# Decoder step on one NeuronCore: where the norm's second statistics, the lower halves of split operands and the convolution's first and last steps stand

## The chip, the cores and the metric

The kernel runs on one core of a Trainium2 chip. The metric is the device time of one execution in microseconds, the median of the runs shown. TensorE (PE), VectorE (DVE), ScalarE (ACT), GpSimd (POOL) and SyncE (SP) each take their instructions in order and wait for each other through semaphores.

## The reference

One inference step of a four-layer decoder for 512 prompt rows and 64 sample rows (8 x 8), 576 rows of width 1024 in all, in float32. Layer 0 and 3 mix with a gMLP, layer 1 with a convolution module, layer 2 with multi-head latent attention; each mixer and each SwiGLU is followed by a norm with conditioning (adaLN):

```python
for i in range(DEPTH):                       # mixer: gmlp, conv, mla, gmlp
    x = LN(ALPHA * x + g1 * mixer(x * (1 + a1) + s1))
    x = LN(ALPHA * x + g2 * (silu(h @ wg) * (h @ wu)) @ wd)   # h = x * (1 + a2) + s2

def conv_module(h, ctx, ...):
    a = h @ w_pw1 + b_pw1                    # 1024 -> 2048
    a = a[..., :D] * sigmoid(a[..., D:])
    full = concatenate([ctx, a], 1)          # ctx: the last 30 rows
    y = depthwise_conv(full, w_dw) + b_dw    # width 31
    y = silu(layer_norm(y, ln_g, ln_b))
    return y @ w_pw2 + b_pw2, full[:, -30:]
```

`layer_norm` takes mean and variance of each row over its 1024 elements. s1, a1, g1, s2, a2, g2 come from `silu(c) @ ada_w[i]`.

## The kernel before, in words

Activations lie transposed: `xa` holds the residual stream as 8 tiles of 128 features by 576 rows (columns 0 to 511 prompt, 512 to 575 sample). A product works on one half of the rows at a time, 288 columns: half 0, then half 1. Precision comes from splitting: a float32 operand is held as an upper part (`h_hi`, `w_hi`, `a_hi`) and a lower part (`h_lo`, ...), and a product is three matmuls for each of its eight tiles of 128 features: upper x upper, upper weights x lower activations, lower weights x upper activations. A matmul is issued through one helper (`mm`, L977), a transpose through `transposes` (L1086). Weights come by DMA in units of 128 x 1024, issued by SyncE; GpSimd splits them (L884 `w_hi`, L887 `w_lo`).

**A norm** (`down_norm` on each engine; seven in the program have it with the first products of the next stage behind it). TensorE makes the down product's eight output tiles, half 0 and half 1. VectorE adds each to `xa` (`add_norm`, L2316 to L2321), which frees its bank in PSUM. It sums tiles (`sums`, L2327) and their squares (`squares`, L2332), which ScalarE has made (L1791), in two groups of four tiles per half; TensorE adds the partial sums over the partitions by a product with a matrix of ones (in the first half it adds tile 7 from `xa` and `sq` itself). Then ScalarE takes the deviation (L1806, L1808), VectorE takes the reciprocal (L2351) and normalises (L2356, L2358), and ScalarE applies the conditioning and writes `hf` and `h_hi` (L1828). VectorE makes `h_lo` from them: for half 0 in two groups of four tiles (`first_half`, L2382), for half 1 in four pairs of tiles (`second_half`, L2392), after the sample columns (`samples`, L2373; cast L2390).

The next stage begins before the norm is done. `first_four` (TensorE) makes the first four products in parts, as tiles of `h` come: two parts of four tiles in half 0, four parts of two in half 1. Each part waits for its `h_lo`. Within a product all three kinds of matmul alternate tile by tile. After the first product of half 0's last part stands `second_stats`, the statistics of half 1, eight records in the trace (each of these matmuls leaves two). Behind half 0's products come products for the conditioning (`ada_w`), then half 1.

**The convolution** (layer 1): the products of w_pw1 come in pairs of units, one pair a tile (value and gate); after pairs 0 and 1, TensorE turns the conditioning row, the sample states `st_in` (eight groups) and the taps `wd_in`; VectorE copies them out of the banks (`stT` L2723, `wdq` L2730, `wdT` L2732) behind its gates, `ada_coefs` (L2257) and `gbw` (L2715 to L2721). ScalarE adds residuals (L1844, sixteen), and issues the DMAs that spread the taps (`w<-wdq`, L1999) and four shifted copies of each tile (`x<-full`, L2009), eight of them before the next gate. GpSimd makes `diag` from mask and taps (L896) and the samples' products (L913). TensorE then runs, for each tile m of eight: the products of pair m + 2 (while there are any), 64 tap matmuls (L977, `pb<-x,diag`), two transposes for the new state. VectorE adds bias into `yc` (L2765), and accumulates `s_sum`, `s_sq` (L2759). At the end: two `ada_conv` pairs, the convolution's statistics (`conv_stats`; the last tile from `yc`, `sqy` by TensorE) with two pairs inside, four pairs after, and `down_norm` with w_pw2. All of this order is written out by hand; a planner (`plan.product`) only counts how often each unit of weights is used.

## Time and profile before

| | |
|---|---|
| median of 3 runs | 3134.82 us (3131.73 to 3137.52) |
| the profiled execution | 3137.26 us |
| its span | 3135.5 us |
| mean granted TensorE clock | 0.989 of full |
| busy: PE, weight loads, DVE, ACT, POOL | 96%, 89%, 46%, 18%, 48% |
| DMA | 354.80 MB, mean 113 GB/s |

The profile is of one execution; its span lies within that execution's own time, and durations come from it. The granted clock is given as a share of full speed: 1.00 is 2.4 GHz, 0.50 is 1.2 GHz. Where TensorE waits, the bracket of a timeline row says how long it stood idle and what released it; the end of a matmul is modelled, so starts are firmer than ends.

### The profile page before, as it was taken

Reading aid. Unit: us, or ns where it says so; the run is one execution under the profiler, and the core shown is the slowest. Engines: PE = TensorE matmul, PEld = TensorE weight load, DVE = VectorE, ACT = ScalarE, POOL = GpSimd, SP = SyncE. Lnnn points to the kernel's source line nnn. Section 1 sums busy time; section 2 is a strip of 40 time slices with the busy share of each in tenths; the row PEclk is TensorE's granted clock in tenths of the full one; section 3 lists DMA queues with packets and bytes.
Section 4 is the critical chain, followed back from the end, with each engine's and each line's share of the span. In section 5 each row is a group of like instructions: output and inputs, shape, how many; then the busy total and the mean of one; then the engine's idle time right before and its main releaser. Section 6 shows DMA issues by size and latency. Waiting matters only on the chain.

```text
span 3135.5 us, 52792 instructions
## 1 busy us (share of the span) xinstructions
PE 3019.7 (96%) x21984; PEld 2788.6 (89%) x21984; DVE 1426.7 (46%) x2530; ACT 555.7 (18%) x1115; POOL 1502.1 (48%) x889
## 2 busy tenths in 40 slices
PE   6999999999999999999989999999999999999998
PEld 4799999999876699999976688999997999899997
DVE  3153663424654763423566546242364536634233
ACT  2230140000220340000233323000023311400001
POOL 2455445545465345555520045554544464455554
PEclk8999999999999999999999999999999999999999
DMA  6642343232345343424321334333322333222321
GB/s 237 226 121 76 121 169 123 82 121 83 90 117 157 130 173 113 145 91 159 92 61 42 104 125 167 122 132 123 127 68 81 98 89 93 69 84 85 88 82 64
DMA packets 450475, 354.80 MB, mean 113 GB/s; under 512 B 26120, under 2 KB 424832, under 8 KB 437933
## 3 DMA queue, kind: packets, MB, share of 16 engines
q1 hardware_dynamic: 435744, 324.79, 32.8%
q10 hardware_dynamic: 14493, 26.63, 2.8%
q8 instruction: 174, 2.85, 0.4%
q14 instruction: 64, 0.52, 0.1%
HBM read 337.86 MB, written 5.25 MB: 109 GB/s over the span
## 4 chain that ended last, share of the span: by engine, by line
PE 85%; DVE 7%; DVEq 2%; ACT 2%; DMA 1%; issue 1%; SPq 1%; ACTq 0%; POOLq 0%; POOL 0%
PE pb L977 83%; DVE h_lo L2382 1%; DVEq L2333 1%; DVE pb L2351 1%; DMA ada_first<-in_ada_w 1%; DVE part L2332 1%; DVE xa L2358 1%; ACT h_hi L1828 1%; ACT hf L1828 1%; PE pb L1672 0%; PE pb L1086 0%; DVEq L2357 0%; DVE h_lo L2392 0%; DVE hf L2373 0%; DVE xa L2356 0%
## 5 line engine op out<-in xcount | busy, mean ns | idle before, releaser
L884 POOL TENSOR_SCALAR w_hi<-w_raw 128x1024 fp32r<-128x1024 f32 (+2 forms) x416 | 444.0, 1067 | 1347.1 <-DMA w_raw<-in_ffn_w_up 405.1
L887 POOL TENSOR_TENSOR w_lo<-w_raw,w_hi 128x1024 fp32r<-128x1024 f32 (+2 forms) x416 | 987.2, 2373 | 69.0 <-issue 69.0
L977 PE MATMUL pb<-h_hi,w_hi 128*128 128x288 f32 x3584 | 974.8, 297 | 12.2 <-DVE h_lo L2392 7.0
L977 PE MATMUL pb<-h_lo,w_hi 128*128 128x288 f32 x3584 | 968.2, 295 | 0.0
L977 PEld LDWEIGHTS pb<-h_hi,w_hi 128*128 128x128 f32 x3584 | 674.3, 188 | 23.6 <-DVE h_lo L2392 12.0
L977 PEld LDWEIGHTS pb<-h_lo,w_hi 128*128 128x128 f32 x3584 | 675.1, 188 | 0.3
L977 PE MATMUL pb<-a_hi,w_hi 128*128 128x288 f32 x2176 | 592.8, 297 | 4.7 <-DVE a_lo L2199 3.9
L977 PE MATMUL pb<-a_lo,w_hi 128*128 128x288 f32 x2176 | 587.4, 295 | 0.0
L977 PE MATMUL pb<-h_hi,w_lo 128*128 128x288 f32 x3584 | 561.8, 295 | 0.0
L977 PEld LDWEIGHTS pb<-h_hi,w_lo 128*128 128x128 f32 x3584 | 504.9, 188 | 0.7 <-POOL w_lo L887 0.5
L977 PEld LDWEIGHTS pb<-a_hi,w_hi 128*128 128x128 f32 x2176 | 408.5, 188 | 13.2 <-issue 6.9
L977 PEld LDWEIGHTS pb<-a_lo,w_hi 128*128 128x128 f32 x2176 | 408.9, 188 | 0.7
L2541 DVE TENSOR_TENSOR pr<-pb,sg 128x288 f32<-128x288 f32 x176 | 80.1, 457 | 629.3 <-PE pb L977 601.7
L977 PE MATMUL pb<-a_hi,w_lo 128*128 128x288 f32 x2176 | 344.5, 295 | 0.2
L977 PEld LDWEIGHTS pb<-a_hi,w_lo 128*128 128x128 f32 x2176 | 307.4, 188 | 0.8 <-POOL w_lo L887 0.7
L1885 ACT ACTIVATE sg<-pb 128x288 f32<-128x288 f32 x176 | 72.2, 411 | 1330.6 <-PE pb L977 1330.5
L2317 DVE SCALAR_TENSOR_TENSOR xa<-pb,gate,xa 128x288 f32<-128x288 f32 (+1 forms) x288 | 137.9, 479 | 210.8 <-PE pb L977 210.3
L2199 DVE TENSOR_TENSOR a_lo<-pr,a_hi 128x288 fp32r<-128x288 f32 x176 | 204.6, 1162 | 15.5 <-issue 2.9
L977 PE MATMUL pb<-w_hi,h_hi 128*128 128x256 f32 (+2 forms) x416 | 135.6, 342 | 21.0 <-DVE h_lo L2392 7.9
L2316 DVE TENSOR_TENSOR pb<-pb,gate 128x64 f32<-128x64 f32 x144 | 33.2, 231 | 255.8 <-PE pb L977 254.8
L2197 DVE CAST a_hi<-pr 128x288 fp32r<-128x288 f32 x176 | 129.2, 734 | 16.1
L977 PE MATMUL pb<-w_hi,h_lo 128*128 128x256 f32 (+2 forms) x416 | 132.5, 335 | 0.0
(321 smaller groups left out, 2699.6 us busy)
## 6 DMA issues: line engine op xcount, KB each, us to landing
ada_w<-in_ada_w SPq DMA_DIRECT2D x80, 1024.0 KB, 8.1
w_raw<-in_ffn_w_gate SPq DMA_DIRECT2D x88, 512.0 KB, 3.8
w_raw<-in_ffn_w_up SPq DMA_DIRECT2D x88, 512.0 KB, 3.8
w_raw<-in_gmlp_w_in SPq DMA_DIRECT2D x64, 512.0 KB, 4.0
w_raw<-in_ffn_w_down SPq DMA_DIRECT2D x64, 512.0 KB, 3.8
w_raw<-in_gmlp_w_out SPq DMA_DIRECT2D x32, 512.0 KB, 4.4
w_raw<-in_ffn_w_down SPq DMA_DIRECT2D x32, 384.0 KB, 3.3
w_raw<-in_conv_w_pw SPq DMA_DIRECT2D x24, 512.0 KB, 4.0
```

The source lines that it names most:

```text
L884: nc.gpsimd.tensor_scalar(w_hi[:, s, 0:w], w_raw[:, s, 0:w], 1.0, 1.0, ALU.mult, ALU.mult).then_inc(split_hi, 1)
L887: nc.gpsimd.tensor_tensor(w_lo[:, s, 0:w], w_raw[:, s, 0:w], w_hi[:, s, 0:w].bitcast(F32), ALU.subtract).then_inc(split_lo, 1)
L977: return nc.tensor.matmul(out, lhsT, rhs, start=start, stop=stop)
L1828: last = fn(dst, xa[:, m, h * HALF:h * HALF + w], ACT.Identity, scale=cs[:, t % RING_T, m, 0:1], bias=cb[:, t % RING_T, m, 0:1])
L1885: fn(sg[:, q, :], pb[:, b, 0:HALF], func, **kw).then_inc(sg_ready, 1)
L2197: v.tensor_copy(hi, src)
L2199: return v.tensor_tensor(lo, src, hi.bitcast(F32), ALU.subtract)
L2316: v.tensor_tensor(bt(ps[:, HP:HALF]), bt(ps[:, HP:HALF]), gs, ALU.mult)
L2317: last_ = v.scalar_tensor_tensor(out=y, in0=ps[:, 0:w], scalar=gp, in1=y, op0=ALU.mult, op1=ALU.add)
L2332: v.reduce_sum(part[:, 1, n, half_cols(h)], sq[:, m0:m1, half_cols(h)].rearrange("p m t -> p t m"), AX.X)
L2333: dve.drain().then_inc(part_ready, 1)
L2541: v.tensor_tensor(pr[:, q, :], pb[:, (G.n + 1) % BANKS, 0:HALF], sg[:, q, :], ALU.mult).then_inc(acc_free, 2)
```

## The change

In every norm but the last: VectorE sums tiles 4 to 6 of half 1, not 4 to 7, and does so ahead of `h_lo` of the second group. TensorE adds tile 7 itself from `xa` and `sq`, for which ScalarE squares tile 7 apart. The statistics of half 1 are split: those of the first four tiles stand ahead of the next stage's products, the rest behind the upper pieces of part 0. `first_four` is regrouped: for each part all four products first do two of the three kinds of matmul, and then, in a second round, the third. In all parts but the first of half 0 the third kind is upper weights x `h_lo`, and the start of a part waits only for `h_hi` (counted by `hf_ready`, or `hs_ready` in half 1). At the very first input the same grouping holds.

```diff
+            def second_stats():
+
+
+                mean_p, sq_p = [pb[:, b, 0:HALF] for b in stat_banks[NT.n, 1]]
+                cols = half_cols(1)
+                pe.wait_ge(y_ready, YR.n + 6)
+                mm(mean_p, ones[:], xa[:, 7, cols], False, False)
+                pe.wait_ge(sq_ready, SQ.n + 7)
+                mm(sq_p, ones[:], sq[:, 7, cols], False, False)
                 pe.wait_ge(part_ready, PT.n + 4)
                 mm(mean_p, ones[:], part[:, 0, 1, cols], False, True).then_inc(mean_ready, 1)
                 mm(sq_p, ones[:], part[:, 1, 1, cols], False, True).then_inc(aux_ready, 1)
                 PT.up(4)
-                YR.up(5)
-                SQ.up(7)
+                YR.up(6)
+                SQ.up(8)
                 NT.up()
...
+                if t and h == 0:
+                    second_stats_early()
                 for part_ in range(parts):
-                    if h and part_ % 2 == 0:
-                        pe.wait_ge(h_pair, 2 * t + part_ // 2 + 1)
+                    ks = range(kn * part_, kn * part_ + kn)
+                    lower_last = h or part_
+                    lower_count = ((h_pair, 2 * t + part_ // 2 + 1) if h and part_ % 2 == 0
+                                   else (h_ready, 4 * t + 2 * h + (part_ // 2 if h else part_) + 1))
+                    if h:
+                        pe.wait_ge(hs_ready, 4 * t + part_ + 1)
+                    elif part_:
+                        pe.wait_ge(hf_ready, 6 * t + part_ + 1)
                     else:
-                        pe.wait_ge(h_ready, 4 * t + 2 * h + (part_ // 2 if h else part_) + 1)
+                        pe.wait_ge(*lower_count)
                     for i in range(4):
                         if part_ == 0:
                             if units is not None and i % 2 == 0:
                                 units(i // 2)
                             pe.wait_ge(acc_free, G.n + i + 1)
-                        last = step(i, range(kn * part_, kn * part_ + kn), (G.n + i) % BANKS)
+                        step(i, ks, (G.n + i) % BANKS, "hh", True, False)
+                        step(i, ks, (G.n + i) % BANKS, "lh" if lower_last else "hl", False, False)
+                    if t and h == 0 and part_ == 0:
+                        second_stats()
+                    if lower_last:
+                        pe.wait_ge(*lower_count)
+                    for i in range(4):
+                        last = step(i, ks, (G.n + i) % BANKS, "hl" if lower_last else "lh", False, True)
                         if part_ == parts - 1:
                             last.then_inc(acc_ready, 1)
-                            if t and h == 0 and i == 0:
-                                second_stats()
                 G.up(4)
...
@@ -2388,7 +2466,7 @@
                 dve.wait_ge(hf_ready, HF.up())
                 ms, src = slice(2 * p, 2 * p + 2), hf[:, p // 2, 2 * (p % 2):2 * (p % 2) + 2, :]
                 v.tensor_copy(h_hi[:, ms, SEQ:], src[:, :, HP:])
-                dve.drain()
+                dve.drain().then_inc(hs_ready, 1)
                 v.tensor_tensor(h_lo[:, ms, half_cols(1)], src, h_hi[:, ms, half_cols(1)].bitcast(F32),
                                 ALU.subtract).then_inc(h_ready if p % 2 else h_pair, 1)
...
@@ -2442,11 +2520,12 @@
                 first.normalise(6, KT)
                 for m in range(5, KT):
                     add_norm(e, m, 1)
-                dve.drain().then_inc(y_ready, 1)
+                    if m >= 6:
+                        dve.drain().then_inc(y_ready, 1)
+                sums(1, 4, 7, 1)
+                squares(1, 4, 7, 1, 6)
                 first_half(1)
-                sums(1, 4, 8, 1)
-                squares(1, 4, 8, 1, 6)
-                second = Stats(1, 7)
+                second = Stats(1, 8)
```

(`pieces` is the loop that issues one kind of matmul of one product for the tiles `ks`.)

In the convolution: the taps `wd_in` are turned first; the states are turned inside the third pair, whose products go unit by unit through both halves. VectorE empties the taps, then makes `gbw`, then copies the states. ScalarE issues four shifted copies, the taps' spread, four shifted copies, and then the residuals. The last tile is done in halves: taps of half 0, its statistics, then taps of half 1 and the new state rows in banks of the products' group. Tiles 6 and 7 are summed by TensorE. Three `ada_conv` pairs stand before the last tile's taps, one before the second statistics, four after. ScalarE takes half 1's deviation after four tiles of half 0; the DMAs of the new states go to the start of half 1.

```diff
+                def third_pair():
+
+
+                    for n, s in enumerate(take_units(2)):
+                        for h in range(2):
+                            at_ = G.n + 2 * h + n
+                            pe.wait_ge(acc_free, at_ + 1)
+                            last = product(pb[:, at_ % BANKS, 0:HALF], range(KT),
+                                           lambda k: (s, slice(k * P, (k + 1) * P)),
+                                           (lambda k: h_hi[:, k, half_cols(h)], lambda k: h_lo[:, k, half_cols(h)]))
+                            if n or h == 0:
+                                last.then_inc(acc_ready, 1 + n * h)
+                        if n == 0:
+                            state_turns()
+                    G.up(4)
...
-                state_turns()
+                pe.wait_ge(st_in_full, 48)
+                transposes([(k * CW, wd_in[:, k * P:(k + 1) * P]) for k in range(KT)])
+                third_pair()
                 for m in range(KT):
-                    if m < KT - 2:
+                    if 0 < m < KT - 2:
...
+                    if m == KT - 1:
+                        pe.wait_ge(acc_free, G.n + BANKS)
+                        ada_conv_pairs(3)
                     pe.wait_ge(diag_ready, m + 1)
                     pe.wait_ge(x4_full[m % 2], 16 * QT * (m // 2 + 1))
+                    last = tap_products(pb[:, aux_bank(), :], m, 0, SEQ if m < KT - 1 else HALF)
                     last.then_inc(aux_ready, 1)
                     X.up()
...
-                pe.wait_ge(acc_free, G.n + BANKS)
-                ada_conv_pairs(2)
-                for h in range(2):
-                    conv_stats(h, 2 * (h == 0))
+                    if m < KT - 1:
+                        new_rows(pb[:, aux_bank(), :], m).then_inc(aux_ready, 1)
+                        X.up()
+                conv_stats(0)
+                tap_products(pb[:, G.n % BANKS, :], KT - 1, HALF, SEQ).then_inc(last_tile, 1)
+                new_rows(pb[:, (G.n + 1) % BANKS, :], KT - 1).then_inc(last_tile, 1)
+                ada_conv_pairs(1)
+                conv_stats(1)
                 ada_conv_pairs(4)
...
-                act.wait_ge(bias_ready, 1)
-                residuals(2 * l)
-                act.wait_ge(wd_ready, 1)
-                for q in range(QT):
-                    act.dma_start(w4[:, q], wdq[QC * q:QC * (q + 1)]).then_inc(w4_in, 16)
...
-                for m in range(2):
-                    spread(m)
+                spread(0)
+                act.wait_ge(wd_ready, 1)
+                for q in range(QT):
+                    act.dma_start(w4[:, q], wdq[QC * q:QC * (q + 1)]).then_inc(w4_in, 16)
+                spread(1)
+                act.wait_ge(bias_ready, 1)
+                residuals(2 * l)
...
+                    cols = slice(0, TOK) if m < KT - 1 else half_cols(0)
+                    fn(sqy[:, m % 2, cols], yc[:, m, cols], ACT.Square).then_inc(ysq_ready, 1)
+                deviation("conv", 0)
+                act.wait_ge(yc_ready, KT + 1)
+                fn(sqy[:, (KT - 1) % 2, half_cols(1)], yc[:, KT - 1, half_cols(1)], ACT.Square).then_inc(ysq_ready, 1)
```

How this moves instructions is seen in the built order of each engine. VectorE in the first norm, from the last but one added tile of half 1 on (`pb` is a bank in PSUM, `part` holds the partial sums); before:

```order
L2316 TENSOR_TENSOR pb<-pb,gate 128x64
L2317 SCALAR_TENSOR_TENSOR xa<-pb,gate,xa 128x224
L2321 TENSOR_TENSOR xa<-xa,pb 128x64
L2382 TENSOR_TENSOR h_lo<-hf,h_hi 128x4x288
L2327 TENSOR_REDUCE part<-xa 128x288
L2332 TENSOR_REDUCE part<-sq 128x288
L2345 TENSOR_TENSOR pb<-pb,sqt 128x288
L2347 TENSOR_SCALAR pb<-pb 128x288
L2351 RECIPROCAL pb<-pb 128x288
```

and now:

```order
L2394 TENSOR_TENSOR pb<-pb,gate 128x64
L2395 SCALAR_TENSOR_TENSOR xa<-pb,gate,xa 128x224
L2399 TENSOR_TENSOR xa<-xa,pb 128x64
L2405 TENSOR_REDUCE part<-xa 128x288
L2410 TENSOR_REDUCE part<-sq 128x288
L2460 TENSOR_TENSOR h_lo<-hf,h_hi 128x4x288
L2423 TENSOR_TENSOR pb<-pb,sqt 128x288
L2425 TENSOR_SCALAR pb<-pb 128x288
L2429 RECIPROCAL pb<-pb 128x288
```

The two reduces stand ahead of `h_lo`, and only then come the second half's variance, clamp and reciprocal. TensorE at the second statistics of the same norm, the end of the first product's second part; before:

```order
L977 MATMUL pb<-h_lo,w_hi 128x288
L977 MATMUL pb<-h_hi,w_hi 128x288
L977 MATMUL pb<-h_lo,w_hi 128x288
L977 MATMUL pb<-h_hi,w_lo 128x288 x4
L977 MATMUL pb<-part,ones 128x288 x4
L977 MATMUL pb<-h_hi,w_hi 128x288
L977 MATMUL pb<-h_lo,w_hi 128x288
L977 MATMUL pb<-h_hi,w_hi 128x288
```

and now, from the down product's last piece:

```order
L980 MATMUL pb<-a_hi,w_lo 128x288 x8
L980 MATMUL pb<-part,ones 128x288 x2
L980 MATMUL pb<-h_hi,w_hi 128x288 x4
L980 MATMUL pb<-h_lo,w_hi 128x288 x4
L980 MATMUL pb<-h_hi,w_hi 128x288 x4
L980 MATMUL pb<-h_lo,w_hi 128x288 x4
L980 MATMUL pb<-xa,ones 128x288
L980 MATMUL pb<-sq,ones 128x288
L980 MATMUL pb<-part,ones 128x288 x2
L980 MATMUL pb<-h_hi,w_lo 128x288 x16
L980 MATMUL pb<-h_hi,w_hi 128x288 x4
```

The four matmuls with ones have become two ahead of the products and four behind the upper pieces of part 0; the `h_lo` pieces of part 1 (sixteen, not shown) end half 0. ScalarE at the convolution's start, from the gates of tile 1; before:

```order
L1907 ACTIVATE sg<-pb,par 128x288 x2
L1844 ACTIVATE xa<-xa,ab,ag 128x288 x16
L1999 DMA w_122<-wdq 128x1x64 x4
L2009 DMA x_119<-full 128x1x540 x8
L1907 ACTIVATE sg<-pb,par 128x288 x2
L2009 DMA x_119<-full 128x1x540 x4
```

and now:

```order
L1981 ACTIVATE sg<-pb,par 128x288 x2
L2078 DMA x_119<-full 128x1x540 x4
L2083 DMA w_122<-wdq 128x1x64 x4
L2078 DMA x_119<-full 128x1x540 x4
L1918 ACTIVATE xa<-xa,ab,ag 128x288 x16
L1981 ACTIVATE sg<-pb,par 128x288 x2
L2078 DMA x_119<-full 128x1x540 x4
```

The shifted copies of tile 0 have passed the residuals and the taps' spread, and the residuals stand behind all of them.

## Rows read from the trace of the kernel before

**Rows 1.** The page: busy time of the engines; shares of the chain that ended last.

```profile
PE 3019.7 (96%) x21984; PEld 2788.6 (89%) x21984; DVE 1426.7 (46%) x2530; ACT 555.7 (18%) x1115; POOL 1502.1 (48%) x889
...
PE 85%; DVE 7%; DVEq 2%; ACT 2%; DMA 1%; issue 1%; SPq 1%; ACTq 0%; POOLq 0%; POOL 0%
```

**Rows 2.** TensorE's waits: releaser: us in total, times, longest us.

```profile
PE pb L977 <- DVE h_lo L2392: 14.9, 11, 4.7
PE pb L977 <- DVEq L2333: 13.6, 14, 2.5
PE pb L977 <- DVE h_lo L2382: 8.8, 6, 6.9
...
PE pb L977 <- DVE xa L2321: 4.9, 7, 0.8
...
PE pb L977 <- issue: 3.1, 1, 3.1
PE pb L977 <- DMA ada_conv<-in_ada_w: 3.1, 3, 1.4
...
PE pb L977 <- DVEq L2784: 0.8, 1, 0.8
```

**Rows 3.** Timeline, TensorE, norms: start us, us, operation [idle before <-releaser].

```profile
1578.20 0.39 PE L977 MATMUL pb<-w_hi,h_hi 128*128 128x256 f32 x1 [2.13 <-DVE h_lo L2392]
...
2681.72 0.40 PE L977 MATMUL pb<-h_hi,w_hi 128*128 128x288 f32 x1 [0.55 <-DVE h_lo L2382]
...
2689.07 0.29 PE L977 MATMUL pb<-h_hi,w_hi 128*128 128x288 f32 x1
...
2690.65 1.13 PE L977 MATMUL pb<-part,ones 128*128 128x288 f32 x4
2693.01 1.24 PE L977 MATMUL pb<-part,ones 128*128 128x288 f32 x4 [1.23 <-DVEq L2333]
...
2703.66 0.61 PE L977 MATMUL pb<-h_hi,w_hi 128*128 128x288 f32 x1 [4.68 <-DVE h_lo L2392]
```

**Rows 4.** The same, VectorE, last norm.

```profile
2685.88 2.82 DVE L2382 TENSOR_TENSOR h_lo<-hf,h_hi 128x1152 fp32r<-128x1152 f32 x1
2688.63 2.25 DVE L2327 TENSOR_REDUCE part<-xa 128x288 f32<-128x1152 f32 x1
2690.81 2.12 DVE L2332 TENSOR_REDUCE part<-sq 128x288 f32<-128x1152 f32 x1
2694.31 0.47 DVE L2345 TENSOR_TENSOR pb<-pb,sqt 128x288 f32<-128x288 f32 x1 [1.39 <-PE pb L977]
...
2702.85 0.76 DVE L2392 TENSOR_TENSOR h_lo<-hf,h_hi 128x576 fp32r<-128x576 f32 x1
```

**Rows 5.** Groups by form: busy us, mean ns | idle before.

```profile
L2327 DVE TENSOR_REDUCE part<-xa 128x288 f32<-128x864 f32 x7 | 8.0, 1145 | 0.8
```

**Rows 6.** Stretches: us, busy (x) of PE, PEld, DVE, ACT, POOL, PEclk, DMA share, GB/s.

```profile
877.00:896.00 19.00, 14.56 (x93) 13.72 (x93) 11.32 (x32) 8.90 (x17) 7.78 (x7) 0.82 0.60 158
1014.00:1024.00 10.00, 6.88 (x54) 2.08 (x46) 9.67 (x9) 0.68 (x1) 9.67 (x6) 0.83 0.64 216
1040.00:1048.00 8.00, 6.58 (x30) 3.18 (x31) 5.34 (x8) 5.51 (x10) 0.00 (x0) 0.57 0.27 114
1575.00:1596.00 21.00, 16.85 (x139) 15.51 (x132) 15.69 (x39) 14.73 (x30) 1.57 (x2) 1.00 0.16 38
2702.00:2710.00 8.00, 6.33 (x27) 6.34 (x28) 6.91 (x16) 4.88 (x12) 0.00 (x0) 0.57 0.00 0
```

**Rows 7.** Timeline of the convolution's start, three engines.

```profile
879.48 0.42 PE L1086 MATMUL pb<-ident,st_in 120*128 120x120 f32 x2 [0.62 <-DVE cb L2257]
...
883.20 4.26 ACT L1844 ACTIVATE xa<-xa,ab,ag 128x288 f32<-128x288 f32 x8 [4.80 <-DVEq L2721]
...
883.72 1.86 PE L1086 MATMUL pb<-ident,st_in 120*128 120x120 f32 x8 [3.81 <-DVE stT L2723]
...
891.63 2.34 POOL L896 TENSOR_TENSOR diag<-mask,w 128x256 f32<-128x256 f32 x4 [8.58 <-DMA w<-wdq]
```

More of the change, by code:

```diff
@@ L266, in trunk @@
         gbw = ca("gbw", [P, KT, NC])
-        ci = Place(a_at, size([P, 2, QT, XW]), "conv-in")
+        ci = Place(a_at + size([P, 2, QT, XW]), 2 * size([P, DEC_B, DEC_T, CW]), "conv-in")
         wd_in = ci("wd_in", [CW, D])
@@ L1141, in second_stats, with pieces @@
                 PT.up(4)
-                YR.up(5)
-                SQ.up(7)
+                YR.up(6)
+                SQ.up(8)
                 NT.up()
+            def pieces(out, ks, w_at, a_at, w, wait, start, end, w_moves):
+                for k in ks:
+                    s, cols = w_at(k)
+                    wait(s)
+                    a = a_at(k)
+                    lhsT, rhs = (a, w[:, s, cols]) if w_moves else (w[:, s, cols], a)
+                    last = mm(out, lhsT, rhs, start and k == 0, end and k == KT - 1)
+                return last
             def first_four(t, h, step, units=None):
@@ L1177, in first_halves, with step, w_at @@
                 first_four(t, h, step, None if h else lambda _: slots.extend(take_units(2)))
             def first_tokens(t, h, slots, widths, both):
-                def step(i, ks, b):
+                def step(i, ks, b, kind, start, end):
                     blk, tt = ((0, 2), (0, 3), (0, 4), (1, 2))[i] if h else divmod(i, 2)
                     n = widths[blk]
+                    def w_at(k):
+                        return slots[blk][k // 4], slice(k % 4 * n, (k % 4 + 1) * n)
                     if tt == TT - 1:
-                        if KT - 1 not in ks:
+                        if not end or KT - 1 not in ks:
@@ L1194, in units @@
+                    w, wait = (w_lo, wait_lo) if kind == "lh" else (w_hi, wait_hi)
+                    a_at = token_parts(h_hi, h_lo, both, tt)[kind == "hl"]
+                    return pieces(pb[:, b, 0:n], ks, w_at, a_at, w, wait, start, end, True)
                 def units(blk):
@@ L1453, in state_turns, with tap_products, new_rows @@
                 def state_turns():
-                    pe.wait_ge(st_in_full, 48)
                     for k in range(KT):
                         transposes([(n * 4 * CTX, st_in[:, n, k * P:(k + 1) * P]) for n in range(2)])
-                    transposes([(k * CW, wd_in[:, k * P:(k + 1) * P]) for k in range(KT)])
+                def third_pair():
[11 more added lines that the diff above has]
+                    G.up(4)
+                def tap_products(out, m, c0, c1):
+                    for g in range(TG):
+                        for q in range(QT):
+                            last = mm(out[QC * q:QC * (q + 1), 0:c1 - c0], diag[:, m % 2, q, g, :],
+                                      x4[:, m % 2, q, QT * g + c0:QT * g + c1], g == 0, g == TG - 1)
+                    return last
+                def new_rows(out, m):
+                    pe.wait_ge(full_ready, m + 1)
+                    nc.tensor.transpose(out[0:CTX, 0:P], full[:, m % 3, SEQ:SEQ + CTX], ident[:]
+                                        ).then_inc(taps_done, 1)
+                    return nc.tensor.transpose(out[0:NS, P:2 * P], snew[:, m % 3, :], ident[:])
                 slots = []
@@ L2733, in conv @@
                 dve.drain().then_inc(wd_ready, 1)
-                v.memset(full[:, :, 0:CTX], 0.0)
-                v.memset(full[:, :, CTX + SEQ:SAMPLES], 0.0)
+                v.tensor_tensor(gbw[:], gate[:, 2 * l % RING_T], par[:, C_PW2:C_PW2 + KT].unsqueeze(2)
+                                .to_broadcast([P, KT, NC]), ALU.mult)
+                dve.drain()
+                v.tensor_tensor(ab[:, 2 * l, :], ab[:, 2 * l, :], gbw[:, :, 0], ALU.add)
+                v.tensor_tensor(gbw[:, :, 1:], gbw[:, :, 1:], gbw[:, :, 0:1].to_broadcast([P, KT, NC - 1]),
+                                ALU.subtract)
+                dve.drain().then_inc(bias_ready, 1)
                 v.memset(s_sum[:], 0.0)
                 v.memset(s_sq[:], 0.0)
+                for m in range(KT):
+                    v.tensor_copy(stT[:, m, :], pb[:, aux(), 0:DEC_B * CTX]).then_inc(aux_free, 1)
                 dve.drain()
@@ L2784, in lower @@
                     dve.drain().then_inc(a_ready, 2)
-                first = Stats(0, 1)
-                first.invert()
-                second = Stats(1, 2)
                 for p in range(4):
```

131 lines of the change are left out of this document (69 added, 62 removed).

## The prediction

> **What bounds the kernel now.** I read the page first: busy shares and the chain of waits. TensorE is busy 96% of the span and carries 85% of the chain; VectorE carries 7% of it [rows 1]. So only places where TensorE stands still, or runs at its lower clock, can be won. The second view is the table of TensorE's waits [rows 2]. The named waits that this change can touch are in the norms (the second statistics, L2333; the lower parts h_lo, L2392 and L2382; the banks that xa frees, L2321) and in the convolution (stT, taps that wait for x, ada_conv, L2784). The third is the timeline of one norm, on TensorE [rows 3] and on VectorE [rows 4]: the 2.82 us h_lo of the second group of tiles and two reduces over four tiles, 2.25 and 2.12 us, stand one behind the other before the second statistics can close, at 2693.01. Everything of the second half (deviation, reciprocal, normalising, h_lo) hangs on that, and TensorE, which runs out of first-half products, stands 4.68 us until 2703.66. The fourth is the table of stretches with the granted clock [rows 6]: a stretch loses its length times (1 - clock). 2702 to 2710 at 0.57 lost 3.4 us, behind that 4.68 us stand.
>
> **The norms (seven times).** The waits: seven second-statistics waits, 1.23 us the last [rows 3], 9.3 us in all; the other seven of L2333's fourteen stand elsewhere in the norm and stay; h_lo L2392, 14.9 us in 11 waits; h_lo L2382 without the 6.9 us at the program's start, 1.9 us [rows 2]. Together 26.1 us. A wait costs a little on top: from start to start the stand is longer than its bracket (2690.65 with its four records of 0.24, to 2693.01, is 1.4, not 1.23). I take 0.25 us each, 4.5 us for the 18 that go.
>
> What comes in. (a) TensorE sums tile 7 itself: two matmuls with ones more for the second half, two records each. The four records behind 2693.01 take 1.24 us with the modelled end of the last; start to start I take 0.24 a record [rows 3]: 0.97 us a norm, 6.8 us. This is on the path, since TensorE is the bound. (b) The two early statistics move ahead of part 0. No work is added, and they fill the L2382 wait, 1.9 us in all; where there is none they come from behind it and cost nothing. (c) The bank wait L2321 (4.9 us, seven times) stays: the first product now does two pieces instead of three before it wants the second bank, but starts later by the early statistics; I add 1.1 us. (d) VectorE's reduces cover three tiles, 1.15 us instead of 2.2 each [rows 5], and stand before h_lo of the second group. h_lo of the second group started at 2685.88, behind the last add; from there the two reduces are done at about 2688.2. TensorE starts part 0 at about 2682.3, behind the early statistics, and has 32 records of 0.13 (twelve take 1.58, 2689.07 to 2690.65 [rows 3]), about 1 us of bank wait and two of the new matmuls before it needs them, so to 2688.0: I put 0.2 us of wait, 1.4 us in seven. The squares of tile 7 come right behind those of 4 to 6 on ScalarE, inside that time. mean_ready comes about 5 us sooner, but VectorE then still owes h_lo: free at 2688.2 + 2.8 = 2691.0, where it began the second half's chain at 2694.31 [rows 4]. The chain comes 3.2 us sooner. (e) In the second half the lower parts are asked for last, so a part starts 0.76 us (one h_lo) before it could [rows 4]: 4.0 us in all. TensorE itself arrives about 1 us sooner. So most of the eleven L2392 waits vanish; of the 4.68 about 1.8 is left, of the others together 2.2: 4.0 us.
>
> Balance: 26.1 + 4.5 - 6.8 - 1.1 - 1.4 - 4.0 = 17.3 us. The clock: the 2702 stretch lost 3.4 us [rows 6] and should go with its stand cut to 1.8 us. The first input gains 0.3 us, its lower parts behind the upper. **Norms 21.0 us.**
>
> A 2 us stand need not lower the clock: 1575 to 1596 holds one of 2.13 us [rows 3] at clock 1.00 [rows 6].
>
> **The convolution's start.** TensorE waits 0.62 us for cb and 3.81 us for stT [rows 7], because VectorE makes gates, coefficients and gbw before it empties the banks of the turned states, and 877 to 896 at 0.82 loses 3.4 us [rows 6]. With the states turned inside the third pair's products, with VectorE free for them by then, the waits go: 4.4 + 0.5 for the restarts + 3.4, less 1.0 for the wait that I leave (VectorE must empty the banks of eight turned groups while the third pair's products need theirs): **7.3 us**. The shifts: four x<-full go ahead of w<-wdq, and the sixteen residuals behind both. GpSimd's diag waited 8.58 us for w<-wdq there [rows 7] and TensorE has the third pair's 96 records of 0.13 and the turns, 14 us, before the first taps, so I put this at nothing; if that cover were gone, it would cost what ScalarE's queue is late: eight residuals took 4.26 us [rows 7], so sixteen are 8.5.
>
> **Its end.** Taps of tile 7 waited 3.1 us ("issue", for x), ada_conv 3.1 us in three, L2784 0.8 us [rows 2], with five restarts, 1.2 us; the clock lost 1.7 us (1014 to 1024) and 3.4 us (1040 to 1048) [rows 6]. Three of the ada_conv pairs now stand in the x wait. Waits, restarts and clock are 13.3 us. Against it: eight more records for tile 6's sums, 1.9 us; a wait of about 2.5 us before w_pw2's second half, whose chain on VectorE (second deviation, reciprocal) comes forward less than TensorE does; two more table loads on ScalarE beside that wait, of which I count 0.3 as seen; 1.3 us of small waits around the halved tile. Halving the taps adds no columns, and no price of its own. **7.3 us.**
>
> The sum is 21.0 + 7.3 + 7.3 = 35.6 us. The profiled execution took 3137.26 us (span 3135.5), 2.4 above the median of the three runs, 3134.82; against the median the sum gives **3099 us**. SP's and GpSimd's instructions are not moved.
>
> **Where the trace is silent.** Whether the regrouped pieces keep 0.131 us a record: the bounds are 0.13, the pace of a product's part now (a gain is excluded, since the alternating pieces keep that pace already: those twelve records are of such a product), and 0.24, a record of ones; I take 0.13, since each of those products already ends with a run of four of one kind at that pace. Whether new small waits lower the clock: 0 to 3.4 us a place.
>
> **A rule against one step.** Between 877 and 896 the clock was low beside stands of 0.62 and 3.81 us with only transposes between [rows 6, 7]; the trace cannot say which of them did it. The Trainium skill, "TensorE: Matmul & The Clock Gate", Part 4: PE-mode transpose, says that transposes do not count as a busy TensorE in the same way. By the forecast the clock gain at the conv start is 3.4 us; by that rule sixteen turns could still bring a fall, and nothing of it would come.
>
> **Rivals.**
> 1. *VectorE stays the bound of the second half* (0.17). For: its long operations stand close [rows 4]. If h_lo of the second group and the gates' products delay the chain so that it is 1 us sooner, not 3.2, then L2392 keeps some 11 us instead of 4.0, and the 3.4 us of clock stay: 3099 + 7 + 3.4 = 3109. Against: nothing is added to VectorE's queue and 2.1 us leave it.
> 2. *The clock falls elsewhere* (0.18). The 2.5 us before w_pw2's second half, 1.8 us at 2700 and the conv's turns are candidates, 1.7 to 3.4 us each. One or two: 3102 to 3106; all: 3108.
> 3. *Slower: small waits lower the clock in every norm* (0.04). Place: the first products, now cut by a bank wait, a wait for the reduces and one for h_lo within about 8 us. Before, three ada_conv stands of 3.1 us together [rows 2] had a half-clock stretch beside them, at 1040 to 1048. Price: 3.4 us a stretch of 7 us [rows 6], 24 us in seven norms, which brings 3123; the kernel is slower than before by over 6 us once each norm loses 6 us, that is once each stretch is 12 us long. The Trainium skill, the same page, "A second HAM failure mode: psum-queue depth-cycling", tells of short idle spells between matmul groups that make the clock swing without one long one. Against: each norm has three or more such waits now, and the clock over 2702 is low behind a 4.68 us stand.
> 4. *The statistics do not come sooner* (0.05): second_stats sits in TensorE's queue between products, so if it stands there for ScalarE's squares or the reduces as long as before (1.3 us), 6.8 us of new records buy nothing, and the norms give 3 instead of 21: 3117. With the convolution's new order also failing (its waits moved to tile 0's taps, 14 us back) it is 3131, no change.
>
> **Numbers.** Forecast case 3092 to 3104: 0.56. The range takes in rivals 1 and 2 and, below, the left-over waits all gone: 3087 to 3113. 0.2% is 6.3 us, about what a measurement of this kernel can tell. Faster 0.91 (forecast, rivals 1, 2, most of 4), same 0.05, slower 0.04.
>
> **What would show it.** In the waits table L2333's successor falls from 13.6 to under 6 us, h_lo L2392's from 14.9 to about 4; stT and x waits are gone; matmuls with ones gain 28 records in the norms and 8 in the convolution; a new wait of 2 to 3 us stands before w_pw2's second half; granted clock is 1.00 at 885 to 895, at the conv's end and at the last norm. I am wrong if the second half's h_lo is less than 2.5 us sooner behind the first statistics, if a regrouped product takes over 0.14 us a record, or if new stretches at half clock appear in norms.

## The result: 22 us faster where 36 were forecast, and the profile after

| | before | changed |
|---|---|---|
| median | 3136.17 us (4 runs, 3131.73 to 3138.53) | 3113.72 us (4 runs, 3109.77 to 3117.25) |
| profiled execution's span | 3135.5 us | 3114.0 us |
| mean granted TensorE clock | 0.989 | 0.991 |

The ratio is 0.9938, 95% interval 0.9927 to 0.995: faster by 16 to 23 us. The forecast was 3099, the range 3087 to 3113. The page of the changed kernel, engines and data moved, answers to [rows 1]:

```profile
PE 3020.4 (97%) x22084; PEld 2794.3 (90%) x22084; DVE 1431.8 (46%) x2529; ACT 557.7 (18%) x1125; POOL 1509.5 (48%) x889
```

TensorE's waits, answering to [rows 2] (releaser: us in total, times, longest us):

```profile
PE pb L980 <- DVE h_lo L2460: 7.0, 1, 7.0
...
PE pb L980 <- DVE a_lo L2277: 5.6, 5, 1.4
...
PE pb L980 <- DVEq L2469: 5.2, 4, 2.7
PE pb L980 <- DVE bst L2663: 5.1, 2, 3.0
PE pb L980 <- DVE xa L2399: 5.0, 7, 1.2
...
PE pb L980 <- POOL w_hi L887: 2.3, 5, 0.6
PE pb L1745 <- DMA pgr<-in_cache_krope: 2.3, 1, 2.3
...
PE pb L980 <- DVEq L2411: 2.1, 6, 0.6
PE pb L980 <- DVEq L2880: 1.9, 1, 1.9
PE pb L980 <- DVE pr L2620: 1.4, 4, 0.4
```

The second statistics' wait is gone: L2333's 13.6 us were 9.3 before the second and 4.3 before the first statistics of a half, and the 2.1 us left at L2411 all stand before the first. h_lo L2392's 14.9 us have become 5.2 us for the samples' upper half (L2469); stT's is gone. New are waits for `w_hi` and `pr`, and the waits for `a_lo` grew from 3.9 us in three to 5.6 in five.

The granted clock of some stretches (columns as in [rows 6]):

```profile
880.00:892.00 12.00, 11.81 (x91) 11.25 (x90) 7.72 (x19) 0.51 (x1) 5.34 (x6) 1.00 0.93 252
1020.00:1035.00 15.00, 14.80 (x140) 8.98 (x133) 13.20 (x20) 11.09 (x17) 6.11 (x4) 1.00 0.23 80
1782.00:1788.00 6.00, 4.68 (x29) 4.68 (x30) 2.67 (x5) 2.29 (x7) 3.57 (x2) 0.72 0.94 273
2677.00:2690.00 13.00, 10.31 (x66) 10.07 (x66) 9.68 (x22) 9.06 (x19) 0.00 (x0) 0.87 0.00 1
```

The convolution's start and end run at full clock now. The last norm still loses 13 x 0.13 = 1.7 us, and 1782 to 1788, in the sample attention's page loads, loses 1.7 that it did not lose before.

**Where the time came from.** Starts of the same TensorE operation in two traces, subtracted, give the lead over before; here at the end of each stage (times of before), for the change and for four experiments that are described below:

```
stage end (us in before)         change    e1    e2    e3   e10
 486 first norm, feed-forward      -1.3   0.5   0.0   2.0   1.8
 878 second norm                    1.3   5.1   0.2   5.5   5.0
 908 convolution's start            7.3   9.2   7.6  12.3   4.4
1060 w_pw2, second half            13.8   9.0  14.1  18.8   4.9
1194 third norm                    17.1   8.9  14.5  20.6   6.5
1539 feed-forward, layer 1         15.7   8.9  13.0  19.3   4.9
1591 fourth norm                   20.4  13.7  13.0  23.6   9.1
1866 latent attention              16.6  12.6  11.7  24.0  10.2
2317 fifth norm, feed-forward      17.7  14.7  12.4  26.2  12.5
2404 sixth norm, gMLP's start      19.8  17.2   8.5  28.4  14.9
2770 last norm, feed-forward       22.7  20.5   9.9  34.9  20.8
3093 end                           21.5  18.9   7.5  33.8  18.1
```

The convolution brought 6.0 us at its start and 6.5 up to w_pw2's second half (forecast 7.3 and 7.3). The feed-forward norms (first, third, fifth, last) brought little: -0.2 over the first (from -1.1), and 2.9 over the last where some 7 were expected. And leads are lost where the change touches nothing: 1.4 us at 1194 to 1539, 3.8 in the attention, 1.2 at the end, and 1.1 before the first norm. By these rows the norms brought 16.4 us of 20.7 (21.0 less the 0.3 for the first input), the convolution 12.5 of 14.6, and 7.5 were lost outside both.

### The profile page after: what moved, and what is told of

Its sections match the earlier page's. It is cut to its first block, busy times and chain, and to the rows that moved or that the text cites. A ratio compares the mean times of both kernels' runs of the same rounds, so it can differ in the third digit from the quotient of the medians.

```text
span 3114.0 us, 53016 instructions
## 1 busy us (share of the span) xinstructions
PE 3020.4 (97%) x22084; PEld 2794.3 (90%) x22084; DVE 1431.8 (46%) x2529; ACT 557.7 (18%) x1125; POOL 1509.5 (48%) x889
## 3 DMA queue, kind: packets, MB, share of 16 engines
q8 instruction: 175, 2.87, 0.4%
HBM read 337.86 MB, written 5.25 MB: 110 GB/s over the span
## 4 chain that ended last, share of the span: by engine, by line
issue 33%; PE 30%; POOL 24%; POOLq 10%; DVE 2%; ACT 1%; DVEq 0%; ACTq 0%
PE pb L980 29%; POOL w_lo L890 22%; POOLq L889 10%; POOL prod L916 1%; POOL diag L899 1%; PE pb L1745 0%; PE pb L1702 0%; DVE a_lo L2277 0%; POOLq L945 0%; POOL w_hi L887 0%; POOL yt L946 0%; POOL a_lo L936 0%; DVE xa L2436 0%; DVE pb L2429 0%; PE pb L1624 0%
## 5 line engine op out<-in xcount | busy, mean ns | idle before, releaser
L980 PE MATMUL pb<-h_hi,w_hi 128*128 128x288 f32 x3584 | 946.1, 296 | 10.6 <-DVE xa L2399 3.8
L980 PE MATMUL pb<-h_lo,w_hi 128*128 128x288 f32 x3584 | 927.1, 295 | 0.0
L980 PEld LDWEIGHTS pb<-h_hi,w_hi 128*128 128x128 f32 x3584 | 661.8, 188 | 21.7 <-issue 8.6
L980 PEld LDWEIGHTS pb<-h_lo,w_hi 128*128 128x128 f32 x3584 | 657.6, 188 | 0.0
L2277 DVE TENSOR_TENSOR a_lo<-pr,a_hi 128x288 fp32r<-128x288 f32 x176 | 214.5, 1219 | 13.5 <-issue 0.4
L2275 DVE CAST a_hi<-pr 128x288 fp32r<-128x288 f32 x176 | 145.9, 829 | 16.8 <-issue 0.9
L980 PE MATMUL pb<-w_hi,h_hi 128*128 128x256 f32 (+2 forms) x416 | 122.4, 343 | 15.9 <-DVE h_lo L2460 7.0
L980 PE MATMUL pb<-w_hi,h_lo 128*128 128x256 f32 (+2 forms) x416 | 114.8, 336 | 0.0
```

What stands on the lines that cost most here:

```text
L980: return nc.tensor.matmul(out, lhsT, rhs, start=start, stop=stop)
L2275: v.tensor_copy(hi, src)
L2277: return v.tensor_tensor(lo, src, hi.bitcast(F32), ALU.subtract)
```

## The first norm, read in the changed trace

ScalarE (start us, us, operation [idle before <-releaser]):

```profile
408.20 0.41 ACT L1879 ACTIVATE sqt<-pb 128x288 f32<-128x288 f32 x1 [2.67 <-PE pb L980]
409.84 0.47 ACT L1881 ACTIVATE pb<-pb,epsl 128x288 f32<-128x288 f32 x1 [1.24 <-DVE pb L2425]
415.57 1.28 ACT L1959 ACT_TABLE_LOAD   x1 [5.25 <-PE pb L980]
416.87 0.71 ACT L1959 ACTIVATE sg<-pb 128x288 f32<-128x288 f32 x2
417.46 0.57 ACT L1901 ACTIVATE hf<-xa,cb,cs 128x224 f32<-128x224 f32 x1
```

and VectorE, as it ends the first two normalised tiles, which ScalarE reads first:

```profile
413.23 0.76 DVE L2436 TENSOR_TENSOR xa<-xa,pb 128x576 f32<-128x576 f32 x1
```

In the trace of before, ScalarE:

```profile
411.24 0.41 ACT L1806 ACTIVATE sqt<-pb 128x288 f32<-128x288 f32 x1 [6.83 <-PE pb L977]
...
417.03 0.57 ACT L1828 ACTIVATE hf<-xa,cb,cs 128x224 f32<-128x224 f32 x1 [1.68 <-DVE xa L2358]
```

The statistics came early, as forecast: `sqt` at 408.20, where before it was 411.24. The changed trace is 1.1 us behind before's by then, so counted from the norm's own start they came 4.1 us sooner. But `hf` of the second half (the apply, which writes the operands of the next products) starts at 417.46, and was at 417.03 before: 0.7 us sooner by the same count. Before, it waited for VectorE; now VectorE has the two tiles ready at 414.0, and ScalarE stands 5.25 us for a gate (`sg`), whose product is now finished only in the second round of the last part, with all the others. TensorE at the end of the second half:

```profile
434.85 0.40 PE L980 MATMUL pb<-h_hi,w_hi 128*128 128x288 f32 x1 [0.36 <-DVE pr L2620]
438.83 0.37 PE L980 MATMUL pb<-h_hi,w_hi 128*128 128x288 f32 x1 [0.55 <-POOL w_hi L887]
```

and SyncE's loads and GpSimd's first split of the same timeline:

```profile
433.73 0.38 SPq L728 DMA_DIRECT2D w_raw<-in_ffn_w_up  x1
434.15 0.58 SPq L728 DMA_DIRECT2D w_raw<-in_ffn_w_gate  x1
434.78 1.14 SPq L728 DMA_DIRECT2D w_raw<-in_ffn_w_up  x1
435.96 1.65 SPq L728 DMA_DIRECT2D w_raw<-in_ffn_w_gate  x1
437.63 1.05 POOL L887 TENSOR_SCALAR w_hi<-w_raw 128x1024 fp32r<-128x1024 f32 x1 [25.27 <-DMA w_raw<-in_ffn_w_up]
```

Before, the four weight slots came free one product after another (SyncE's issues at 432.61, 433.41, 434.21, 435.01, the first split at 436.37). Now they come free almost together at the end (the issues start 0.42, 0.63 and 1.18 us apart), and TensorE waits for a bank and then for weights. That pair of waits stands behind every feed-forward norm: 0.36 + 0.55 us in brackets here, 1.2 with the restarts.

## The experiments

Each group of runs was timed beside runs of before of its own. Where a gain over the change or over e3 is given as two numbers, one is the difference of the medians and the other the difference of the distances to before.

**e1 and e2: one half of the change each.** The diff's hunks of the norms alone (`second_stats`, `first_four`, `pieces`, ScalarE's squares, VectorE's order in `down_norm`), and all others alone.

> The kernel before with the norms' part of the change alone. In the two traces the lead over before grows by about 16 us across the convolution and by only some 6 us across all norms together, where 21 were forecast. If the two parts are independent, this kernel gains 5 to 8 us (about 3129). If the small gain at the norms is an artefact of the convolution's new order upstream (weights and clock in other places), it gains 15 us or more (3121 or less).

Measured: 3118.44 us beside 3133.75 for before on that chip, ratio 0.9951 (0.9937 to 0.9964).

> The kernel before with the convolution's part alone. Independent parts: a gain of 14 to 17 us (about 3121), with the sum of this and the norms' part equal to the whole change. If the gain in the convolution needs the norms' part (its first products, its statistics), it stays under 11 us.

Measured: 3128.32 (before 3133.75), ratio 0.9987 (0.9978 to 0.9996). So 15.3 and 5.4 us, and the sum, 20.7, is about the whole; but the split is not the one that the traces led me to expect. In e2's trace the convolution does bring 14.1 us (in the table), and 6.6 of them are lost behind it. In e1's, 4.0 us come at the convolution's start, which this kernel does not touch. I come back to both.

**e3 and e4: the last part of each half, product by product.**

```diff
+                    whole = part_ == parts - 1
+                    if whole:
+                        pe.wait_ge(*lower_count)
                     for i in range(4):
...
+                        if whole:
+                            last = step(i, ks, (G.n + i) % BANKS, "hl", False, True)
+                            if part_ == parts - 1:
+                                last.then_inc(acc_ready, 1)
...
+                    if whole:
+                        continue
```

> The changed kernel, but in the last part of each half the four products are finished one after the other instead of in two rounds. Theory A (the second round is the fault: all four products, their PSUM banks and their weight slots come free together at its end; ScalarE's first gates wait for that, and the second half's apply stands behind them in its queue): 5 to 9 us faster than the changed kernel, about 3106; the waits for pr, POOL's w_hi after the norms (0.65 and 0.84 us, four times) vanish, and apply of half 1 starts about 2 us sooner behind the statistics. Rival B (the added records and the early statistics on TensorE's path are the fault, the order of the pieces is not): within 1.5 us of the changed kernel.

Measured: 3103.38 (before 3133.75), ratio 0.9904 (0.9889 to 0.9919). That is 30 us under before and 8 to 10 under the change, and theory A's signs are there. ScalarE in the first norm:

```profile
406.65 0.41 ACT L1888 ACTIVATE sqt<-pb 128x288 f32<-128x288 f32 x1 [2.67 <-PE pb L980]
410.87 1.28 ACT L1968 ACT_TABLE_LOAD   x1 [2.10 <-PE pb L980]
412.16 0.41 ACT L1968 ACTIVATE sg<-pb 128x288 f32<-128x288 f32 x1
414.05 0.41 ACT L1968 ACTIVATE sg<-pb 128x288 f32<-128x288 f32 x1 [1.47 <-PE pb L980]
414.35 0.56 ACT L1910 ACTIVATE hf<-xa,cb,cs 128x224 f32<-128x224 f32 x1
```

Apply follows the statistics by 7.7 us, not 9.3. The waits for `pr` and `w_hi` are out of the table of TensorE's waits, and the last norm's stand fell from 2.69 to 1.69 us.

> As e3, and the two early statistics stand behind the first product's first pieces, where TensorE waits for the next bank (1.46 us in the first norm). Theory A and B both: since 0.73 us of records move into a wait in seven norms, 3 to 5 us faster than e3. If the bank wait is set by VectorE alone and something else is late behind it, nothing.

Measured: 3104.15 (before 3133.75), ratio 0.991 (0.9895 to 0.9926), no different from e3. The early statistics moved into the bank wait bought nothing that can be measured; their place is not what cost the time.

**e7 and e8: the same, in one half only** (`h == 0 and ...`, `h == 1 and ...`).

> As e3, but only in the first half's last part. It makes the first gates' products ready sooner, which stand ahead of the second half's apply on ScalarE. If that queue is what counts: apply of half 1 some 2 us sooner behind the statistics, the 2.99 us stand in the last norm under 1.5 us, and 3 to 5 us of the 10 won over the changed kernel. The waits for pr and w_hi behind half 1 stay.

> As e3, but only in the second half's last part, which frees weight slots and banks one by one. If the slots are what counts: the 0.65 and 0.84 us waits in the four feed-forward norms vanish, 4.5 to 6 us won over the changed kernel; the 2.99 us stand in the last norm stays.

Measured, beside 3133.21: e7 3110.32, ratio 0.9933 (0.992 to 0.9945); e8 3105.44, ratio 0.9911 (0.9897 to 0.9925). The second half, where weight slots and banks are freed, is worth some 5 to 8 us over the change (27.8 us under before, against 22.4); in e8 the waits for `w_hi` and `pr` are gone and the longest wait for the samples' upper half (L2469 in the change) is still 2.7. The first half, ScalarE's queue, is worth little by itself (22.9 under before), though in e7's trace that stand does fall to 1.7 us and the two waits stay. So of the two ways in which the second round hurts, the slots and banks seem to weigh more; the intervals of e7, e8 and e3 are too wide to split the 10 us cleanly.

**e5 and e6: second traces** of before and of e2.

> The kernel before, unchanged, for a second trace of it. If the 7 us that the convolution's part won up to the end of the convolution (14 us) and lost again behind it are luck of single executions (TensorE's clock falls after one 3 us stand and not after another), this trace differs from the first one stage by stage by 1.7 us or multiples of it, and where its clock is low differs too. If stands decide alone, both traces have the same stretches.

> The convolution's part alone, unchanged from e2, for a second trace. Luck: the lead behind the convolution (14.1 us at its end) is lost in other places than in e2 (there 1.5 us in layer 1's feed-forward part, 2.9 in the sample attention's page loads, 3.5 before the last gMLP, 2.4 at the end). A real give-back: the same places lose the same amounts.

One execution each: 3133.34 and 3130.23 us. Both expectations were half right. The two traces of before differ by up to 5.4 us at one place and 4.0 at the end, most of it in where the clock is low: 3.4 us were lost at 1040 to 1047 in one and 1.7 in the other, nothing at 2371 in one and 1.7 in the other. But e6 loses its lead at the same places as e2 (leads 14.9, 16.2, 14.6, 11.6, 8.2, 7.1 at the stage ends 1060, 1194, 1539, 1866, 2404, 3093), and in like amounts but for the latent attention, 3.0 against 1.3. The give-back is real. Three lines of the waits of e2:

```profile
PE pb L979 <- DVE a_lo L2234: 6.6, 6, 1.3
...
PE pb L979 <- DVE bst L2619: 5.3, 2, 3.9
...
PE pb L1703 <- DMA pgr<-in_cache_krope: 2.4, 1, 2.4
```

Against before these are 2.7 us (a_lo), 0.9 (bst) and 1.6 (page loads) more; the last two stands are now long enough that the clock fell behind them in both traces, which before's did not in the first. How an a_lo wait arises is seen at the end of layer 1's feed-forward part in the changed kernel:

```profile
1485.73 2.38 POOL L890 TENSOR_TENSOR w_lo<-w_raw,w_hi 128x1024 fp32r<-128x1024 f32 x1 [0.16 <-issue]
1485.80 2.62 DVE L2277 TENSOR_TENSOR a_lo<-pr,a_hi 128x288 fp32r<-128x288 f32 x1
...
1488.48 0.41 PE L980 MATMUL pb<-a_hi,w_hi 128*128 128x288 f32 x1 [1.09 <-DVE a_lo L2277]
```

and at the same place of before:

```profile
1502.36 1.27 DVE L2199 TENSOR_TENSOR a_lo<-pr,a_hi 128x288 fp32r<-128x288 f32 x1
```

VectorE's last `a_lo` takes 2.62 us: it starts 0.07 us into GpSimd's `w_lo` and ends 0.31 behind it. Before, it took 1.27: it started 0.09 us into the `w_hi` split (1502.27 to 1503.32) and ended 0.31 behind that. Where GpSimd is idle it takes 0.46. Which of the two it meets is set by where GpSimd stands in its round; I did not find what moved GpSimd there, and made no run that moves it alone.

**e10: the mended norms without the convolution's part.**

> The norms' part alone with the last part of each half whole: e3 without the convolution's part. If the convolution's part is worth little in the whole program (5 us alone in e2): 4 to 7 us slower than e3, about 3109. If its 12 to 14 us at the place arrive once the norms are mended: 11 to 14 us slower than e3, about 3116.

Measured: 3119.27 (before 3132.49), ratio 0.9958 (0.9944 to 0.9972), 16 to 17 us slower than e3, more than the 11 to 14 expected. So the convolution's part, worth 5.4 us over before, is worth at least its full place value over the mended norms (13.3 us in e3's column); and the mending, worth 8 to 10 us over the change, is worth nothing over e1 (13.2 us under before, against 15.3). The table says where: e10 leads e1 in the feed-forward norms, and falls behind by 4.6 us at the convolution's start. VectorE there, in e1:

```profile
874.43 0.23 DVE L2759 TENSOR_TENSOR gbw<-gate,par 128x72 f32<-128x72 f32 x1
...
874.82 0.22 DVE L2763 TENSOR_TENSOR gbw<-gbw 128x64 f32<-128x64 f32 x1
```

and in e10:

```profile
874.53 1.07 DVE L2768 TENSOR_TENSOR gbw<-gate,par 128x72 f32<-128x72 f32 x1
...
875.77 2.37 DVE L2772 TENSOR_TENSOR gbw<-gbw 128x64 f32<-128x64 f32 x1
```

In e1 the weight slots come free late, GpSimd starts its splits at 875.81, behind `gbw`, and `gbw` takes 0.45 us; in before and e10 GpSimd works beside it, `gbw` takes 3.4 us, and TensorE stands 3.8 us for stT. The late slots that cost 1.2 us in each feed-forward norm happen to save 4 us here: e1 and e10 differ in the last part of each half alone. The convolution's part takes `gbw` out of TensorE's way for good, so with it that saving is no longer there to lose.

**e9: no lower part last.** `whole = h or part_`: every part but the first waits for its h_lo again.

> As e3, but each product's pieces stay together in every part but the first of half 0, so nothing is gained by asking for h_lo last. If waiting only for h_hi is worth what the forecast said (0.76 us a stand, 4 us in all, most of it in the gMLP norms and the last norm): 3 to 5 us slower than e3. If the chain's gain alone does it: within 1.5 us of e3.

Measured: 3106.87 (before 3132.49), ratio 0.9918 (0.9905 to 0.9932): 3.5 us over e3 by the medians, 4.8 by the distance to before. The intervals overlap, so this alone does not show it; size and sign are those of the forecast's 4.0.

**e12: tile 7 back with VectorE.**

```diff
-                mm(mean_p, ones[:], xa[:, 7, cols], False, False)
-                mm(sq_p, ones[:], sq[:, 7, cols], False, False)
...
-                sums(1, 4, 7, 1)
-                squares(1, 4, 7, 1, 6)
+                sums(1, 4, 8, 1)
+                squares(1, 4, 8, 1, 7)
```

> As e3, but VectorE sums four tiles again (2.2 us a reduce, not 1.15) and TensorE does not add tile 7. TensorE has 0.97 us less in each of seven norms, VectorE's chain starts 2.1 us later. If the records are the dearer side in the feed-forward norms: 2 to 5 us faster than e3. If the chain is: the statistics' wait grows by 1 us a norm and the stands of the gMLP norms and of the last by 2 us, 4 to 8 us slower.

Measured: 3124.76 (before 3132.49), ratio 0.9974 (0.9965 to 0.9983): 21 to 23 us slower than e3, far past what I expected. The first norm:

```profile
408.18 1.94 PE L980 MATMUL pb<-part,ones 128*128 128x288 f32 x4 [2.82 <-DVEq L2416]
```

TensorE now asks for the second statistics after 32 records and not after 60, so the longer reduces are in full view: 20.2 us of that wait in seven norms (none in the change), with the clock low at five of the seven. Low stretches cost this trace 15.4 us and e3's 6.8. The four records of 0.24 us buy three times their price, at this place of the statistics. Four tiles by VectorE with the second statistics asked for later, as in before, is a rival that no run here tries.

**e11: the gates apart.** As e3, and ScalarE writes the first two tiles of half 1 between the two first gates, VectorE likewise.

> As e3, and in the feed-forward norms ScalarE writes the first two tiles of half 1 between its two first gates, VectorE makes their samples and h_lo between the two gated products. If ScalarE's queue still holds the second half up (in e3 apply stands behind the gate that waits for the fourth product): the stand in the last norm falls from 1.99 to under 1 us, 1 to 2 us faster than e3. If VectorE's chain is what is last there: no change.

Measured: 3100.86 (before 3132.49), ratio 0.9901 (0.9886 to 0.9916). The stand in the last norm is gone in its trace:

```profile
2670.78 0.54 PE L980 MATMUL pb<-h_hi,w_hi 128*128 128x288 f32 x2 [0.18 <-DVEq L2482]
```

So ScalarE's queue did hold that half up. Counted from the first statistics of the same norm, the first `h_lo` of half 1 starts 38.1 us behind them in before, 36.2 in the change and 33.6 here in the first norm; 38.1, 35.6 and 32.7 in the last. By the medians e11 is 2.5 us faster than e3, by the distance to before 1.3; the intervals overlap. Both beat the change; their medians are the lowest of all.

## Why the prediction was wrong

- **The waits that go**: right. The second statistics' own wait went from 9.3 us to nothing (forecast 1.4 left), L2392's from 14.9 to 5.2 (forecast 4.0 left); bank wait 5.0 (forecast 6.0), new records 0.24 us each. That the other seven of L2333's waits stay was not quite so: 4.3 us became 2.1, since the one of 2.5 us at 1092 is not in this trace (in e3's it is).
- **"The chain comes 3.2 us sooner"**: this is one of the two places that failed. The statistics did come sooner, and VectorE's reciprocal too (410.35 against 413.31, 4.1 us from the norm's own start; `h_lo` took 1.44 us where 2.82 was counted), but I counted VectorE's queue alone. ScalarE's queue holds two gates ahead of apply, and they wait for products whose last pieces the change itself had moved to the end. Rival 1 named the gates' products, as work on VectorE and not as something that ScalarE stands for. The first `h_lo` of half 1 came 1.9 us sooner behind the first statistics in the first norm, 1.8 in the second and 2.4 in the fifth, which meets the prediction's own sign of being wrong (under 2.5). In the last norm, where 1.8 us was to be left and the clock to stay up, 2.69 us and 1.7 us of clock were seen; with the queue mended (e11) the stand is 0.18.
- **What is missing from the sum**: the regrouping signals four products at once. I priced what each part waits for, and not what waits for its end: weight slots, banks, gates. It cost 1.9 + 1.4 us of new waits behind the four feed-forward norms and, with the chain, 8 to 10 us (e3), most of the miss of 13 to 15 us. By the table of leads e3's norms bring 22.1 us, where 20.7 were forecast and the change has 16.4. Part of e3's lead in its trace is chance: it has 5.1 us less of low clock in the attention than the change, and e4 and e11, with the same last part, have the long stretch at 1590 again. The medians, and not that trace, carry the 8 to 10.
- **The clock**: low stretches between 70 and 3080 us cost 20.5 us in before and 11.9 in the change, a gain of 8.5 where the sum had 3.4 + 3.4 + 5.1 = 11.9. The stretches that I named went, but for half of the last norm's; a new one came at 1783 and the attention's grew by 1.7 us. Rival 2 held in part. The Trainium skill, "TensorE: Matmul & The Clock Gate", Part 4: PE-mode transpose, says that a transpose does not count as a busy TensorE in the same way; that the turned states lower the clock by that, no run here shows: 880 to 892 of the changed kernel has sixteen of their records between products at 1.00.
- **The convolution**: start 6.0 for 7.3, end 6.5 for 7.3 and the 1.9 us wait before w_pw2's second half for 2.5. Nearly right at its place; what is lost behind it (6.6 us in e2) was no term of the sum, and stays open: it lies in `a_lo` waits, page loads and the clock, and no run moves one of them alone. The stand at gbw was read as VectorE's order, and it was also GpSimd's work beside it.
- **Rivals 1, 3 and 4**: half 1 was held up as rival 1 has it, with L2392's successor at 5.2 us and not 11, and by ScalarE's queue and not VectorE's; no norm fell to half clock as a whole; the statistics came early.

## What to carry to other kernels

When pieces of several products are regrouped so that a late operand is asked for last, ask first who waits for each product's end. Keep the last part product by product: e3, which does so, keeps the gain and loses the new waits. And a part of a change that is measured alone may show another part's accident: here the convolution's part and the whole last part were each worth 0 to 5 us alone and 8 to 17 us beside the other.

## What the runs showed of the hardware

- Some of VectorE's operations take two to ten times as long beside some of GpSimd's: `gbw` 0.22 against 2.37 us, `a_lo` 0.46 against 2.62. What counts is where they start. Over the fourteen traces all 748 `a_lo` (128x288) that started inside a `w_lo` ended 0.31 or 0.32 us behind its end, after 1.92 to 2.65 us, and the 1245 that started inside no operation of GpSimd took 0.46. The six `gbw` of 128x64 that started inside a `w_lo` ended 0.08 us behind it (0.22 alone). So such an operation gets about its own time, less 0.15 us, once `w_lo` is done. The products `pr` out of PSUM took 0.46 inside a `w_lo` too (948 of them), and the reduces over three tiles 1.12 to 1.17. A VectorE duration from one trace is a duration beside a given neighbour.
- The same shortened the second `h_lo` of a norm, which took 2.82 to 2.85 us in each of the seven before and takes 1.36 to 1.44 now; the forecast had counted 2.82. Before, it started 0.8 us into a `w_lo` and ended 1.2 us behind it, its 1.36 less 0.15, all seven times. In the change it starts ahead of `w_lo`, beside `w_hi` alone, or in the last 0.23 us of a `w_lo`; the first norm, before and now:

```profile
402.51 2.41 POOL L887 TENSOR_TENSOR w_lo<-w_raw,w_hi 128x1024 fp32r<-128x1024 f32 x1 [0.16 <-issue]
403.30 2.84 DVE L2382 TENSOR_TENSOR h_lo<-hf,h_hi 128x1152 fp32r<-128x1152 f32 x1
```

```profile
405.28 2.39 POOL L890 TENSOR_TENSOR w_lo<-w_raw,w_hi 128x1024 fp32r<-128x1024 f32 x1 [0.16 <-issue]
407.44 1.44 DVE L2460 TENSOR_TENSOR h_lo<-hf,h_hi 128x1152 fp32r<-128x1152 f32 x1
```

- Whether the clock falls behind one stand of TensorE is not fixed by its length in the middle range. Over the fourteen traces, stands (start to start) between 70 and 3080 us had a stretch at 1.2 GHz begin during them or within 2 us behind in 23 of 23 cases from 3.9 us up, in 11 of 15 from 3.2 to 3.7, in 21 of 35 from 2.5 to 3.2, and in 1 of 17 from 2.2 to 2.5; of 28 from 1.9 to 2.2 us long 8 had, some of them with other stands close by. Behind the same stand the same kernel's clock fell in one trace and not in the other (3.26 us at 2370 in before's first, 2.87 at 2365 in its second). That frequent short idle spells of TensorE between groups of matmuls can make the clock swing is what the Trainium skill says in "TensorE: Matmul & The Clock Gate" (A second HAM failure mode: psum-queue depth-cycling). The trace of before agrees at 1038 to 1045, where stands of 1.8, 2.0 and 1.6 us had 3.4 us lost beside them; a stand of 2.15 us that stood alone, before w_pw2's second half, had a low stretch in four traces of ten.
- The spread of one kernel's times (3109.77 to 3117.25 for the change) goes with its clock: 0.993 at the lowest, 0.990 at the highest.
